# Retention's output gate token-major in wide matmuls, and the convolution's steps dealt by chunk over six projections

## What is computed

```python
def mixer_sublayer(u, ...):
    q, k, v, g_ret, c_in, gates = jnp.split(u @ w_in, cuts, axis=-1)   # 1024, 1024, 2048, 2048, 2048, 2048 columns
    q = rotary(q.reshape(bsz, seq, 4, 256), cos, sin) * 256 ** -0.5
    k = rotary(k.reshape(bsz, seq, 4, 256), cos, sin)
    v = v.reshape(bsz, seq, 4, 512)
    o = head_group_norm(chunk_retention(q, k, v), ret_gn_g)            # mean and variance over a head's 512 columns
    y_a = (jax.nn.silu(g_ret) * o) @ w_ret_out
    a, b = jnp.split(c_in, 2, axis=-1)
    c = a * jax.nn.sigmoid(b)
    c = causal_dwconv(c, conv_dw_w, conv_dw_b)                         # 31 taps on each of 1024 channels
    c = jax.nn.silu(layer_norm(c, conv_ln_g, conv_ln_b))
    y_b = c @ w_conv_out + b_conv_out
    g_a, g_b = jnp.split(jax.nn.sigmoid(gates + b_gate), 2, axis=-1)
    return (g_a * y_a + g_b * y_b) @ w_mix_out
```

## Time and profile before

| | |
|---|---|
| median of 3 runs | 2103.97 us (2103.52 to 2105.73) |
| profiled execution | 2104.84 us, span 2103.2 us |
| TensorE (PE) busy | 2073.7 us, 99% |
| VectorE (DVE) busy | 1666.5 us, 79% |
| ScalarE (ACT) busy | 1061.2 us, 50% |
| GpSimd (POOL) busy | 260.0 us, 12% |
| granted TensorE clock | 0.998 of full speed |

### The profile page before, as it was taken

One profiled execution on the slowest core, in us unless ns is written; L12 is line 12 of the kernel. 1 busy time (PEld: TensorE's weight loads), 2 busy tenths in 40 slices (PEclk: granted clock), 3 DMA queues, 4 the chain that ended last, 5 costly groups with the idle time before them and its releaser, 6 DMA issues.

```text
span 2103.2 us, 40039 instructions
## 1 busy us (share of the span) xinstructions
PE 2073.7 (99%) x16378; PEld 2015.8 (96%) x16378; DVE 1666.5 (79%) x2449; ACT 1061.2 (50%) x1282; POOL 260.0 (12%) x176
## 2 busy tenths in 40 slices
PE   9999999999999999999999999999999999999998
PEld 9999999999989999989999999999988999989998
DVE  8897888788778877898986768768698996758765
ACT  6886444357754434355545445444346445445442
POOL 0212055000005500001202001100000301100100
PEclk9999999999999999999999999999999999999999
DMA  6553545453335455453554444445453555534543
GB/s 261 191 194 131 187 181 183 165 214 141 121 116 185 156 184 208 169 179 142 199 182 181 160 142 173 180 159 208 181 181 141 182 186 182 176 137 166 189 150 117
DMA packets 58281, 361.66 MB, mean 172 GB/s; under 512 B 6736, under 2 KB 9360, under 8 KB 21136
## 3 DMA queue, kind: packets, MB, share of 16 engines
q1 hardware_dynamic: 58128, 359.48, 47.9%
HBM read 358.37 MB, written 1.08 MB: 171 GB/s over the span
## 4 chain that ended last, share of the span: by engine, by line
PE 88%; DVE 6%; ACT 2%; issue 2%; DMA 1%; POOL 1%; SPq 0%; DVEq 0%; ACTq 0%; POOLq 0%
PE acc L639 72%; PE acc L638 7%; DVE w_lo L1191 2%; ACT w_hi L2054 1%; PE acc L754 1%; PE acc L755 1%; PE acc L756 1%; DVE arena L1413 1%; PE acc L959 1%; PE pA L1008 0%; DVE arena L1456 0%; DMA raw<-in_wide 0%; PE pB L1032 0%; PE pD L1119 0%; PE pB L1119 0%
## 5 line engine op out<-in xcount | busy, mean ns | idle before, releaser
L639 PE MATMUL acc<-in_hi,w_hi 128*128 128x256 f32 x4656 | 1306.2, 286 | 16.9 <-issue 12.1
L639 PE MATMUL acc<-in_hi,w_lo 128*128 128x256 f32 x4656 | 1292.7, 283 | 0.1
L639 PE MATMUL acc<-in_lo,w_hi 128*128 128x256 f32 x4656 | 1230.2, 283 | 0.0
L2054 ACT CAST w_hi<-raw 128x2048 fp32r<-128x2048 f32 (+1 forms) x341 | 615.4, 1805 | 667.5 <-PE acc L639 587.0
L1191 DVE TENSOR_TENSOR w_lo<-raw,w_hi 128x2048 fp32r<-128x2048 f32 (+1 forms) x341 | 738.8, 2167 | 233.2 <-ACT w_hi L2054 231.6
L639 PEld LDWEIGHTS acc<-in_hi,w_hi 128*128 128x128 f32 x4656 | 891.8, 192 | 25.8 <-issue 22.4
L639 PEld LDWEIGHTS acc<-in_hi,w_lo 128*128 128x128 f32 x4656 | 891.9, 192 | 0.6 <-DVE w_lo L1522 0.3
L639 PEld LDWEIGHTS acc<-in_lo,w_hi 128*128 128x128 f32 x4656 | 854.9, 192 | 1.2 <-issue 1.0
L2654 POOL TENSOR_TENSOR in_lo<-arena,in_hi 128x256 f32 (+2 forms) x112 | 145.2, 1296 | 1217.7 <-ACT in_hi L2514 515.7
L1835 DVE SCALAR_TENSOR_TENSOR arena<-arena,cols 128x256 f32<-128x256 f32 x480 | 200.3, 487 | 0.0
L2664 POOL TENSOR_TENSOR arena<-arena 128x256 f32<-128x256 f32 x44 | 81.9, 1861 | 387.9 <-ACT arena L2336 387.9
(11 more groups left out here) (293 smaller groups left out, 1628.1 us busy)
## 6 DMA issues: line engine op xcount, KB each, us to landing
raw<-in_wide SPq DMA_DIRECT2D x285, 1024.0 KB, 4.8
raw<-in_narrow SPq DMA_DIRECT2D x64, 704.0 KB, 4.0
arena<-cs_rows SPq DMA_DIRECT2D x16, 256.0 KB, 4.6
arena<-in_mem SPq DMA_DIRECT2D x3, 1024.0 KB, 6.9
x<-in_x SPq DMA_DIRECT2D x4, 256.0 KB, 6.5
raw<-in_wide SPq DMA_DIRECT2D x2, 512.0 KB, 5.8
tables<-in_tables SPq DMA_DIRECT2D x1, 1024.0 KB, 15.4
arena<-cs_rows SPq DMA_DIRECT2D x16, 64.0 KB, 5.3
```

Of the source, the lines that this page charges most:

```text
L639: return mm(outs[m], w[:, k, at], moving[:, c, :], start=start, stop=stop)
L2054: copy(w_hi[g % 2][:, 0:n], raw[g % RAW][:, 0:n]).then_inc(hi_ready, 1)
```

## The change

ret_g becomes a `tok_pair` projection like ret_v, with its weights laid out for it. A head's gate (two units) then stands token-major in two PSUM banks. ScalarE takes silu in place there, behind every second unit. VectorE's `ret_gate`, now by head, multiplies the two banks into `o_tok` in place and frees them. Only then does TensorE transpose (`ret_turn(l, u - 3)` behind unit u, the last three behind the first three units of gates), and ScalarE applies the gain as it copies pB to `ret_y` (`ret_turned`), followed by `ret_high` and GpSimd's subtraction, which come one unit later than before. In gates ScalarE waits for the last `ret_gate` before its first sigmoid.

The convolution's taps are replaced by a running count of steps, `conv(l, n)`: 2, 2 and 3 steps in glu's last three units, 6 in each unit of ret_q, 8 and 0 in turn in ret_k, 8 in a unit of ret_v (16 in two of them), 8 and 6 in turn in ret_g, 7 in each unit of gates (8 in the last), and 8 in ret_out. In all they are 248, as before.

```diff
@@ segments
-              ("ret_v", "tok_pair", DC // 2, 8, MIXER_AT), ("ret_g", "feat", DC, 8, MIXER_AT),
+              ("ret_v", "tok_pair", DC // 2, 8, MIXER_AT), ("ret_g", "tok_pair", DC // 2, 8, MIXER_AT),
@@ build
-        ret_s = view(13296, 2, 2, T)
+        rg_silu = sem("rg_silu")
+        def gates_freed(l, h):
+            return [s.base for s in segs if s.name == "ret_g"][l] + 2 * h + 2
@@ TensorE
             def ret_turn(l, u):
                 h, p = divmod(u, 2)
-                pe.wait_ge(ro_a, RH * l + h + 1)
+                pe.wait_ge(acc_free, gates_freed(l, h))
                 if 8 * l + u:
                     pe.wait_ge(gated_v, 8 * l + u)
...
                         if u == 0:
                             ret_values(l, RH - 1)
-                        else:
-                            ret_turn(l, u - 1)
+                        elif u >= 3:
+                            ret_turn(l, u - 3)
...
-                    project("gates", after=lambda u, j: ret_turn(l, 7) if j == 0 else None)
+                    project("gates", after=lambda u, j: ret_turn(l, 5 + j) if j < 3 else None)
@@ VectorE
-            def conv_tap(l, tap, between=None):
-                for c in range(DC):
-                    if between and c == DC // 2:
-                        between()
+            conv_at = [0] * LAYERS2
+            def conv(l, n):
+                for _ in range(n):
+                    tap, c = divmod(conv_at[l], DC)
+                    conv_at[l] += 1
                     if c < DC - 1:
                         E.settle(DC - 2)
-                    elif not (l == 0 and isinstance(tap, int) and tap == 0):
+                    elif l or tap:
                         dve.wait_ge(dw_v, tap + CTAPS * l)
...
-            def ret_gate(l, u):
-                n = 8 * l + u
-                dve.wait_ge(rt_mm, n + 1)
-                dve.wait_ge(acc_free, [t.base for t in segs if t.name == "ret_g"][l] + u + 1)
-                for c in range(2):
-                    ins = stt(out=ret_y[:, 2 * u + c, :], in0=pB[:, c * T:(c + 1) * T], scalar=wcol(f"ret_gain{l}", 2 * u + c),
-                              in1=ret_s[:, u % 2, c, :], op0=ALU.mult, op1=ALU.mult)
-                    E.mark(ins) if c == 0 else ins.then_inc(gated_v, 1)
+            def ret_gate(l, h):
+                n = RH * l + h
+                dve.wait_ge(rg_silu, n + 1)
+                dve.wait_ge(ro_a, n + 1)
+                banks = wide_banks(gates_freed(l, h) - 2)
+                for t in range(TT):
+                    y = o_tok[h][:, :, t, :]
+                    ins = tt(y, banks[t].rearrange("p (a n) -> p a n", a=2), y, ALU.mult)
+                    E.mark(ins) if t == 0 else ins.then_inc(acc_free, 2)
...
                     def between(u, j, banks):
                         glu(u, j, banks)
+                        if j >= 5:
+                            dve.wait_ge(acc_free, glu_base + j)
+                            conv(l, (2, 2, 3)[j - 5])
...
-                        project(n, rotary, lambda u, j, banks: conv_tap(l, u // 2 + o) if j % 2 == 0 else None, early=True)
+                        project(n, rotary, lambda u, j, banks: conv(l, (8 if j % 2 == 0 else 0) if o else 6), early=True)
...
                     def values(u, j, banks):
...
-                        tap = 4 + j + (j > 3) + (j > 5)
-                        conv_tap(l, tap, (lambda: ret_root(l, 2)) if j == 7 else None)
-                        if j in (3, 5):
-                            conv_tap(l, tap + 1)
+                        conv(l, 4)
+                        if j == 7:
+                            ret_root(l, 2)
+                        conv(l, 12 if j in (3, 5) else 4)
...
                     def gated(u, j, banks):
                         if j == 1:
                             ret_root(l, 3)
-                        if j:
-                            ret_gate(l, u - 1)
-                        conv_tap(l, j + 14)
+                        conv(l, 6 if j % 2 else 8)
+                        if j % 2:
+                            ret_gate(l, j // 2)
...
-                    def last_gated(u, j, banks):
-                        if j == 0:
-                            ret_gate(l, 7)
-                        conv_tap(l, j + 22)
-                    project("gates", None, last_gated)
+                    project("gates", None, lambda u, j, banks: conv(l, 8 if j == 7 else 7))
@@ ScalarE
-            def ret_silu(l, seg, u):
...
-                fn(ret_s[:, u % 2], acc[(seg.base + u) % 4][:].rearrange("p (m l) -> p m l", m=2), ACT.Silu).then_inc(acc_free, 1)
+            def ret_silu(l, h):
+                act.wait_ge(unit_done, gates_freed(l, h))
+                for t, bk in enumerate(wide_banks(gates_freed(l, h) - 2)):
+                    ins = fn(bk, bk, ACT.Silu)
+                    E.mark(ins) if t == 0 else ins.then_inc(rg_silu, 1)
+            def ret_turned(l, u):
+                act.wait_ge(rt_mm, 8 * l + u + 1)
+                for c in range(2):
+                    ins = fn(ret_y[:, 2 * u + c, :], pB[:, c * T:(c + 1) * T], ACT.Copy, scale=wcol(f"ret_gain{l}", 2 * u + c))
+                    E.mark(ins) if c == 0 else ins.then_inc(gated_v, 1)
...
+                        if u % 2:
+                            ret_silu(l, u // 2)
                         if u == 1:
                             ret_scaled(l, 3)
-                        ret_silu(l, ret_g, u)
-                        if u >= 2:
-                            ret_high(l, u - 2)
+                        if u >= 3:
+                            ret_turned(l, u - 3)
+                            ret_high(l, u - 3)
                     def gates(u, j, banks):
+                        if j == 0:
+                            act.wait_ge(acc_free, gates_freed(l, RH - 1))
...
-                        if j < 2:
-                            ret_high(l, 6 + j)
+                        if j < 3:
+                            ret_turned(l, 5 + j)
+                            ret_high(l, 5 + j)
```

More of the change, by code:

```diff
@@ L1819, in glu @@
                    ).then_inc(acc_free, 1)
-            def conv_tap(l, tap, between=None):
-                for c in range(DC):
-                    if between and c == DC // 2:
-                        between()
+            conv_at = [0] * LAYERS2
[3 more added lines that the diff above has]
+                    conv_at[l] += 1
                     if c < DC - 1:
                         E.settle(DC - 2)
-                    elif not (l == 0 and isinstance(tap, int) and tap == 0):
+                    elif l or tap:
                         dve.wait_ge(dw_v, tap + CTAPS * l)
-                    src, w = c_pad[:, c, bass.ds(tap, T)], wcol(f"dw_w{l}", tap * DC + c)
-                    if isinstance(tap, int) and tap == 0:
+                    src, w = c_pad[:, c, tap:tap + T], wcol(f"dw_w{l}", tap * DC + c)
+                    if tap == 0:
                         ins = ts(cvo[:, c, :], src, w, wcol(f"dw_b{l}", c), ALU.mult, ALU.add)
@@ L1872, in run @@
                     E.settle()
+                    glu_base = take.base()
                     def between(u, j, banks):
                         glu(u, j, banks)
+                        if j >= 5:
+                            dve.wait_ge(acc_free, glu_base + j)
+                            conv(l, (2, 2, 3)[j - 5])
                         if l == 0 and j == 4:
@@ L1916, in conv_end @@
                         if j == 0:
-                            conv_tap(l, 30)
+                            conv(l, DC)
+                            assert conv_at[l] == CTAPS * DC
                         if j == 1:
@@ L2791, in arrays @@
         wide += [tiles(glu, np.arange(16).reshape(2, 8).T.reshape(-1)), tiles(w[:, 0:2048]), wide_tiles(w[:, 2048:4096]),
-                 tiles(w[:, 4096:6144]), tiles(w[:, 8192:10240]), tiles(v["w_ret_out_2"][l])]
+                 wide_tiles(w[:, 4096:6144]), tiles(w[:, 8192:10240]), tiles(v["w_ret_out_2"][l])]
         kv = v["w_xkv_2"][l]
```

## The result

The changed kernel takes 2109.59 us (median of 12 runs, 2108.57 to 2110.94) against 2104.25 us of the kernel before (12 runs beside it): 1.0026 of it, 95% interval 1.0018 to 1.0034. It is slower by 5.3 us; the interval lies clear of 1, and its lower end, 0.18%, is just under the 0.2% that the prediction took for the least that can be told. The profiled execution has a span of 2107.9 us against 2103.2. Lines have moved: the narrow matmul is now L643 and the wide one L642, ScalarE's cast L2062, the low half L1195, the rotation L1811 to L1816, a convolution step L1840, the gate's product L1864, GpSimd's subtraction L2673.

A forecast was written before the change was run, and what follows sets the result against it. TensorE, busy 99% of the span, was taken as the bound, with VectorE a second bound just beneath. Terms -4.8 + 8.3 + 2.3 = +5.8 us on the median 2103.97 gave 2109.8, range 2103.0 to 2113.0.

The forecast's parts named there:

- Part 2: ret_q and ret_k: the new dealing of convolution steps backs VectorE up and makes TensorE wait, +8.3 us in two layers.
- cover: Delay VectorE may have before TensorE waits: about 1.05 us in ret_q and ret_k, about 1.55 in ret_g and gates.
- the 0.18 of the settle: ret_q: the rotation must wait for the chunk's last step, now a marked one, costing 0.18 us a unit.
- the 0.395 of a step: VectorE's time for one convolution step, 0.395 us, making a ret_q unit with six steps 6.64 before the settle.
- The steps in glu: glu's last three units take 2, 2 and 3 steps in VectorE's idle time: nothing, up to 1 us without that cover.
- Part 1: Gate projection: sixteen units go from 48 narrow to 24 wide matmuls, -4.8 us at ret_v's rate.
- Rival D: Gate projection: the wide units gain nothing and stay at 5.77 us, giving 2114.6; chance 3%.
- Part 3: ret_g and gates: steps behind the low half, exposed to GpSimd's subtraction, delay VectorE; +2.3 us in two layers.
- a wait that I had named and priced at nothing: Gates: seventh transposition waits for ScalarE's sixth copy behind product, table load and two sigmoids, about 3 us, counted as hidden.
- A: ret_g, gates or rotation: GpSimd exposure stays small or the settle is free, +1.2 to +4, 2105 to 2108; chance 27%.
- B: ret_q: VectorE keeps up, so only matmuls and old gates waits count, -7.1, 2096.9; chance 5%.
- C: Transpositions: TensorE waits at each for ScalarE's copy of the last, 0.5 us x 16, 2118; chance 5%.

The follow-up runs named there:

- e3: Changed kernel with the wait at the rotation's head no longer counting the convolution's marked steps behind the rotation's own last marked instruction: 2107.93 us.
- e10: Changed kernel with 5 convolution steps instead of 6 in each ret_q unit, the four freed steps moved to ret_v's units 0 and 2: 2106.67 us.
- e4: Changed kernel with VectorE's gate product put back directly behind the low half, ahead of the unit's convolution steps: 2105.99 us.
- e5: Changed kernel with 4 steps in every ret_q and ret_k unit, the rest redealt, the shorter rotation wait, and the gate product ahead of the steps: 2095.89 us.
- e6: Changed kernel with GpSimd's subtraction in ret_g cut to one column of 256 per chunk, so part of the result is missing: 2105.92 us.
- e8: Kernel before, with its narrow gate, given 4 steps in every ret_q and ret_k unit and the shorter rotation wait: 2100.84 us.
- e9: Changed kernel with ScalarE's copy of the transposed result and its cast moved ahead of the sigmoids in gates' first three units: 2108.89 us.

## Why the prediction was right

The forecast was 2109.8 us and 5.8 above the kernel before; the measurement is 2109.59, 5.3 above.

**Part 2, the dealing: right in mechanism and size.** A ret_q unit of VectorE is 6.82 us, as worked out; the seven unit ends take 45.33 us against "some 45.4". The rotations of q1, q2, q3, k0, k1 and k2 start 0.99, 2.05, 3.12, 4.19, 6.04 and 4.56 us late, against 1.0, 2.0, 3.1, 4.2, 6.1 and 4.6, counted from 857.31 at 5.76 a unit. The worst of them less the 5.01 us that TensorE lost is a cover of 1.03, against 1.05. The first three ends stay at 5.76 because the backlog is still within the cover; then the units lose 1.0, 1.1, 1.1 and 1.9. e3 confirms the 0.18 of the settle, e10 the 0.395 of a step and the exchange of one to one. The steps in glu were priced at nothing: glu's last unit ends at 851.61, 6.51 us after the one before, and ret_q's first takes 5.76 (to 857.37), both as in the kernel before, so they are.

**Part 1, the wide matmuls: 0.32 instead of 0.30 a unit.** The casts of 978.63 and 984.01 are 5.38 us apart, and the first of them started 0.06 late, behind other work of ScalarE. The unit is thus 5.44 us, so 16 units give 5.1 us and not 4.8. Something is lost again: a transposition and the wide unit behind it take 5.93, which is 0.49 over 5.44 and not the 0.42 of the earlier trace rows. It isn't the wide unit ahead that makes it dearer: in e4, e5 and e6 the transposition behind ret_g's last unit, with a narrow unit to follow, costs 0.43 (6.19 less 5.76). The extra is in the first wide matmul behind a transposition (in the changed kernel 1001.93, with the next at 1002.24: 0.31 us where others are 0.23 apart). Rival D is refuted by the casts and by e8. With it goes the estimate from the Trainium skill, TensorE: Matmul & The Clock Gate, section Back-to-back issue gap: a gain of 0.05 us a unit, where the trace has 0.32.

**Part 3, ret_g and gates: the sum near, its terms not.** I put the loss at 2.3 us a layer, from a backlog of VectorE alone. Measured are 1.85, in two parts. The low halves that VectorE makes behind units 3 to 6 start 0.36, 1.25, 1.72 and 2.61 us behind the ends of their casts, close to my 0.4, 1.4, 1.9 and 2.8. There the forecast fails: it has a hit in every unit, that is, steps that GpSimd's subtraction makes 1.03 longer, and unit 6 has none. The backlog had by then moved VectorE's product to 1005.12, and the subtraction of 1005.17 ran beside the product and cost nothing. So the next low half (1011.71) is 2.07 late and not 3.3, and that behind gates' first unit (1018.52) 1.81, or 2.7 with the 0.87 that TensorE had lost by then, and not 3.9. VectorE's steps and the subtractions stand like this (VectorE first, then GpSimd):

```profile
1001.71 3.49 DVE L1840 SCALAR_TENSOR_TENSOR arena<-arena,cols 128x256 f32<-128x256 f32 x6
1005.12 1.28 DVE L1864 TENSOR_TENSOR arena<-acc,arena 128x512 f32<-128x512 f32 x2
1006.32 2.30 DVE L1195 TENSOR_TENSOR w_lo<-raw,w_hi 128x2048 fp32r<-128x2048 f32 x1
1008.54 3.24 DVE L1840 SCALAR_TENSOR_TENSOR arena<-arena,cols 128x256 f32<-128x256 f32 x8
```

```profile
1000.24 2.69 POOL L2673 TENSOR_TENSOR in_lo<-arena,in_hi 128x512 fp32r<-128x512 f32 x1 [3.72 <-ACT in_hi L2528]
1005.17 1.30 POOL L2673 TENSOR_TENSOR in_lo<-arena,in_hi 128x512 fp32r<-128x512 f32 x1 [2.24 <-ACT in_hi L2528]
1012.10 3.04 POOL L2673 TENSOR_TENSOR in_lo<-arena,in_hi 128x512 fp32r<-128x512 f32 x1 [5.63 <-ACT in_hi L2528]
```

Six steps behind the low half take 3.49 us, 1.03 more than 2.46: the price of a hit was right. The eight steps of unit 6 (1008.54) take 3.24, no more than the 3.25 of the earlier trace rows. Beside L1864, one of whose inputs is in PSUM, the subtraction is at its shortest (1.30) and the product as long as elsewhere. That is as the Trainium skill, SBUF — State Buffer, section Who interferes with whom, has it. The backlog costs 0.87 us, at the first unit of gates, whose low half is the one 2.61 late. The cover is thus 1.74; I had 1.55.

The other 0.98 is a wait that I had named and priced at nothing: "by my times that delay falls into the 2.3 already counted". The chain of waits there:

```profile
1017.40 1.21 DVE arena L1864 x2
...
1018.67 1.28 ACT L2556
...
1019.97 0.48 ACT arena L2556
1020.44 0.37 ACT arena L2557
1020.81 0.74 ACT arena L2522 x2
1021.55 0.14 issue
1021.68 0.63 PE pB L1036 x4
```

The last product of VectorE releases ScalarE, which loads its table, takes two sigmoids and only then copies pB; the seventh transposition of TensorE waits for that copy. It was a wait of its own: the backlog had let TensorE go at 1008.72, and no later low half was late enough to hold it, so there was nothing for it to hide behind. My two errors, a backlog loss too large by 1.4 and this chain too small by 0.98, cancel down to 0.45 a layer. That is luck: this part of the sum came near with one of its two waits missing. Both waits have one root all the same, the hits of GpSimd, which make the product late as well: e6 and e4 remove both.

**The sum again, from what was measured, two layers:** -5.1 for the wide units, +8.3 for the dealing, 2 x (1.85 - 1.14) = +1.4 for ret_g and gates, and +0.6 for the eight wide units behind a transposition: +5.2. The first two units of ret_g gained 0.28 and 0.14 us a layer where a wide unit gives 0.32, which is +0.4 again. By casts the mixers are 5.5 longer. The forecast had -4.8, +8.3 and +2.3. The dealing, the largest term, is the one that was right by its own working.

**The rivals.** A (2105 to 2108) supposed that GpSimd's share stays small or that the settle is free. Neither holds: e3 and e6 put the two at 1.7 and 3.7 us. What A had right is that a subtraction can fall where it costs nothing, as at 1005.17. B, that VectorE keeps up in ret_q, is refuted by the casts; a step costs 0.40 us (e10), not under 0.25. Its time is reached by another way: e5, with fewer steps there and no waits in gates, has 2095.89. C, that TensorE waits for ScalarE's copy at every transposition: it does so at one in eight.

**What stays open.** The medians differ by 5.3 us and the profiled spans by 4.7; 0.3 of the difference lies ahead of the first mixer and 0.5 at the end, outside all that was changed, and I have not followed it. Why a wide matmul behind a transposition is slower, and why ret_g's first two units gain less than the others, was not tried.

## What to carry to other kernels

Where a second engine feeds the first in order, write down for each unit how long it takes and how much delay the first one bears. As long as the sum of the surpluses is within that cover an uneven dealing is free, and beyond it each microsecond is lost. What counts is the work in the stretch that has no room, not the total: the mixer has 248 steps in every kernel here, but the change put 40 of them into ret_q and ret_k where 32 had stood. A unit there has room for (5.76 - 4.27) / 0.395 = 3.8 steps, and the cover bears the rest of four. 32 steps dealt as four a unit cost nothing (e5), dealt as 8 and 0 in turn 0.87 us a layer, and 40 cost 5.0. When an instruction is moved, ask what it shielded: VectorE's product from PSUM, between two operations that read only SBUF, was the cover against GpSimd. And a wait that is said to fall into another one has to be placed on the time axis next to it; two waits in different units can add, as here.

## What the runs showed of the hardware

Beside GpSimd's subtraction of 128x512 VectorE loses in either order of starting. If the subtraction is issued during a low half, it ends 1.14 to 1.16 us after the low half, whenever it started (988.38, 993.31, 1000.24 and 1012.10 with lengths of 1.34, 3.21, 2.69 and 3.04 us), and the steps behind are 1.03 longer. If it starts first, it is VectorE's low half that grows: 3.10 us in e9, and 2.83 in the changed kernel at 1024.03, instead of 2.28:

```profile
1024.03 2.83 DVE L1195 TENSOR_TENSOR w_lo<-raw,w_hi 128x2048 fp32r<-128x2048 f32 x1 [0.47 <-ACT w_hi L2062]
```

A VectorE instruction that waits for the end of the one just before it costs 0.18 us more than one that doesn't (e3: 0.92 us a layer over five units). Matmuls in a row with a weight load each are 227 ns apart with 512 columns (5.44 / 24) and 120 with 256 (5.76 / 48), so the wide form does the same columns in 0.944 of the time.
